# A two-layer mixer and a DiT-like block on one core: wider modulation sums, sums moved between the down rows, and products of constants at layer ends

## What is computed

```python
for l in range(2):                                   # first block
    h = x @ w_in[l]; ...                             # two attentions, gates
    x = layer_norm(ALPHA * x + merged @ w_out[l])
mod = silu(c) @ mod_w[i] + mod_b[i]                  # 9 vectors of 1024 per layer
h = x * (1 + scale) + shift                          # modulate
y = 0.5 * ((a * silu(g)) @ wo)                       # half FFN; a, g = h @ wi
x = layer_norm(ALPHA * x + gate * y)
```

## Time and profile before

| | |
|---|---|
| Median of 3 runs | 1699.57 us (1698.55 to 1700.25) |
| The profiled execution's own time | 1696.36 us |
| Its span, first to last instruction | 1694.6 us |
| PE busy | 1601.3 us (94%) |
| DVE busy | 1207.7 us (71%) |
| ACT busy | 802.3 us (47%) |
| Mean granted clock of TensorE | 0.971 |

### The profile page before, as it was taken

One profiled execution on the slowest core, in us unless ns is written; L12 is line 12 of the kernel. 1 busy time (PEld: TensorE's weight loads), 2 busy tenths in 40 slices (PEclk: granted clock), 3 DMA queues, 4 the chain that ended last, 5 costly groups with the idle time before them and its releaser, 6 DMA issues.

```text
span 1694.6 us, 23800 instructions
## 1 busy us (share of the span) xinstructions
PE 1601.3 (94%) x7635; PEld 1311.9 (77%) x7635; DVE 1207.7 (71%) x1849; ACT 802.3 (47%) x1242; POOL 140.1 (8%) x205
## 2 busy tenths in 40 slices
PE   6989989989889999999999798999999999989997
PEld 5877778877678878888788457887888878878876
DVE  6877888877887775677757766777487765475545
ACT  5565535455444444444534465444354443254442
POOL 1100001100011110011100011111001110000000
PEclk9999988999989999999999899999999999999999
DMA  8763448743568888588858105988768885466551
GB/s 313 270 208 128 150 152 310 249 169 112 175 219 267 275 270 233 163 280 275 228 181 243 50 1 173 308 275 270 206 212 275 276 232 176 124 177 196 184 183 55
DMA packets 200497, 349.41 MB, mean 206 GB/s; under 512 B 11188, under 2 KB 128236, under 8 KB 199900
## 3 DMA queue, kind: packets, MB, share of 16 engines
q1 hardware_dynamic: 174668, 252.90, 47.2%
q0 software_dynamic: 25744, 95.43, 17.6%
HBM read 347.21 MB, written 1.08 MB: 206 GB/s over the span
## 4 chain that ended last, share of the span: by engine, by line
PE 86%; DVE 8%; issue 3%; ACT 2%; DMA 0%; SPq 0%; DVEq 0%; ACTq 0%
PE acc L558 25%; PE acc L560 25%; PE acc L559 25%; DVE w_lo L1455 2%; PE score L682 2%; PE turn L886 1%; PE acc L794 1%; PE score L973 1%; PE score L670 1%; PE score L774 1%; DVE att_work L2007 1%; PE turn L783 1%; PE score L838 1%; DVE wide L1783 0%; PE score L577 0%
## 5 line engine op out<-in xcount | busy, mean ns | idle before, releaser
L1455 DVE TENSOR_TENSOR w_lo<-raw,w_hi 128x1024 fp32r<-128x1024 f32 (+1 forms) x490 | 586.0, 1200 | 294.3 <-ACT w_hi L1087 287.7
L1087 ACT ACTIVATE w_hi<-raw 128x1024 fp32r<-128x1024 f32 (+1 forms) x490 | 508.2, 1042 | 563.8 <-PE acc L560 561.4
L558 PE MATMUL acc<-w_hi,xT_hi 128*128 128x512 f32 (+1 forms) x1456 | 586.8, 403 | 23.1 <-DVE xT_lo L1502 8.5
L560 PE MATMUL acc<-w_hi,xT_lo 128*128 128x512 f32 (+1 forms) x1456 | 574.6, 395 | 0.0
L559 PE MATMUL acc<-w_lo,xT_hi 128*128 128x512 f32 (+1 forms) x1456 | 574.1, 394 | 0.0
L558 PEld LDWEIGHTS acc<-w_hi,xT_hi 128*128 128x128 f32 x1456 | 279.4, 192 | 83.1 <-issue 25.7
L560 PEld LDWEIGHTS acc<-w_hi,xT_lo 128*128 128x128 f32 x1456 | 278.6, 191 | 59.2
L559 PEld LDWEIGHTS acc<-w_lo,xT_hi 128*128 128x128 f32 x1456 | 279.6, 192 | 54.6
L458 POOL DMA_DIRECT2D mod_raw<-in_mod_w x144 | 104.0, 723 | 963.5 <-DVE mod_run L1575 777.4
L558 PE MATMUL acc<-w_hi,hT_hi 128*128 128x512 f32 x440 | 174.3, 396 | 0.8 <-DVE hT_lo L1916 0.8
L560 PE MATMUL acc<-w_hi,hT_lo 128*128 128x512 f32 x440 | 173.6, 395 | 0.0
(11 more groups left out here) (259 smaller groups left out, 1266.0 us busy)
## 6 DMA issues: line engine op xcount, KB each, us to landing
raw<-in_ffn_wi SPq DMA_DIRECT2D x220, 512.0 KB, 5.0
mod_raw<-in_mod_w POOLq DMA_DIRECT2D x144, 512.0 KB, 4.4
raw<-in_ffn_wo SPq DMA_DIRECT2D x110, 512.0 KB, 4.8
raw<-in_w_in SPq DMA_DIRECT2D x72, 512.0 KB, 5.2
raw<-in_w_out SPq DMA_DIRECT2D x16, 512.0 KB, 4.5
raw<-in_attn_wqkv SPq DMA_DIRECT2D x16, 512.0 KB, 4.6
wide<-in_b_merge POOLq DMA_DIRECT2D x4, 1024.0 KB, 8.3
raw<-in_w_branch_a SPq DMA_DIRECT2D x8, 512.0 KB, 4.2
```

Source lines behind the costliest of these rows:

```text
L558: nc.tensor.matmul(dst, xh, wh, start=start, stop=False)
L560: return nc.tensor.matmul(dst, xl, wh, start=False, stop=stop)
L1087: nc.scalar.activation(w_hi[:, i % SPLIT_SLOTS, 0:n], raw[:, s, i % 2 * PIECE:i % 2 * PIECE + n], ACT.Copy).then_inc(hi_ready, 1)
L1455: nc.vector.tensor_tensor(w_lo[:, i % SPLIT_SLOTS, 0:n], raw[:, i // 2 % RAW_SLOTS, i % 2 * PIECE:i % 2 * PIECE + n], w_hi[:, i % SPLIT_SL ...
```

## The change

Three parts, all on PE:

1. Every modulation sum multiplies by 48 columns of ones in place of one. The 48 results are equal, and the next product overwrites 47 of them, so that each column that is read holds its own sum. The bank, the count of products and the loads of weights stay.
2. In the first two FFNs the 24 kept sums no longer stand behind the last down row. Four of them follow each of the down rows 11 to 16.
3. A helper `keep_busy(b, n)` issues n products of 128 x 128 constants (`ident` by `ones`) into a free bank, and nobody reads them. At the start of both layers and of the first FFN: 5 ahead of the wait for tile 0, 10 ahead of the wait for tile 1, 5 behind the turn. In the third and fifth FFN, in `project_first`: 6 ahead of the turn of tile 0, 11 behind it, 6 ahead of the turn of tile 1. No such products stand at the start of the fourth FFN and of the Fourier mixing.

```diff
@@ turn @@
                     if tile_ready and g == 0:
+                        if wait[t]:
+                            keep_busy("acc0", wait[t])
                         tile_ready()
@@ project_first @@
+                if not kept:
+                    keep_busy("score0", 6)
                 slots, after = [], [turn_tile(0)]
                 if kept:
                     kept_sums(KEPT_EARLY, MOD_KEPT)
+                else:
+                    keep_busy("score0", 11)
...
                             if i == 2:
+                                if not kept:
+                                    keep_busy("score0", 6)
                                 after.append(turn_tile(1))
@@ new @@
+            def keep_busy(b, n):
+                landed(b)
+                for _ in range(n):
+                    nc.tensor.matmul(bank[b][:, 0:P], ident[:], ones[:], start=True, stop=True)
@@ mod_sum; the same in kept_sums @@
-                        m = nc.tensor.matmul(dst[:, 4 * i + j:4 * i + j + 1], acc[:, j * P:j * P + P], ones[:, 0:1],
+                        m = nc.tensor.matmul(dst[:, 4 * i + j:4 * i + j + SUM_COLS], acc[:, j * P:j * P + P], ones[:, 0:SUM_COLS],
@@ the loop over layers @@
-                after = turn(lambda t, k: x[:, t, k * P:k * P + P], x_tile)
+                after = turn(lambda t, k: x[:, t, k * P:k * P + P], x_tile, wait=(5, 10))
+                keep_busy("acc0", 5)
@@ ffn, down rows @@
                     m.then_inc(piece_done, 1)
+                    if mods and not by_tile and 0 <= k - KEPT_FROM < MOD_KEPT:
+                        kept_sums(k - KEPT_FROM, k - KEPT_FROM + 1)
...
-                if mods:
-                    kept_sums(0, KEPT_EARLY if by_tile else MOD_KEPT)
+                if mods and by_tile:
+                    kept_sums(0, KEPT_EARLY)
@@ the second block @@
-            after = ffn(turn_x(), True, turn_ctx_in, by_tile=False)
+            after = turn_x(wait=(5, 10))
+            keep_busy("acc0", 5)
+            after = ffn(after, True, turn_ctx_in, by_tile=False)
```

More of the change, by code:

```diff
@@ L77 @@
 KEPT_EARLY = 2
+SUM_COLS = 48
+KEPT_FROM = 11
 ACC = ["acc0", "acc1", "acc2", "acc3"]
@@ L560, in product, with turn @@
                 return nc.tensor.matmul(dst, xl, wh, start=False, stop=stop)
-            def turn(src, tile_ready=None, group_ready=None, groups=range(4)):
+            def turn(src, tile_ready=None, group_ready=None, groups=range(4), wait=(0, 0)):
                 order = [(t, g) for t in range(NT) for g in groups] if tile_ready else [(t, g) for g in groups for t in range(NT)]
@@ L681, in kept_sums @@
                     for j in range(4):
-                        m = nc.tensor.matmul(bank["score1"][:, 4 * i + j:4 * i + j + 1], mod_kept[:, i, j * P:j * P + P], ones[:, 0:1],
+                        m = nc.tensor.matmul(bank["score1"][:, 4 * i + j:4 * i + j + SUM_COLS], mod_kept[:, i, j * P:j * P + P], ones[:, 0:SUM_COLS],
                                              start=True, stop=True)
@@ L930, in ffn, with turn_x @@
                         m.then_inc(first_done, 1)
-                if mods:
-                    kept_sums(0, KEPT_EARLY if by_tile else MOD_KEPT)
-                return after
-            def turn_x():
-                return turn(lambda t, k: x[:, t, k * P:k * P + P], x_tile)
+                if mods and by_tile:
+                    kept_sums(0, KEPT_EARLY)
+                return after
+            def turn_x(wait=(0, 0)):
+                return turn(lambda t, k: x[:, t, k * P:k * P + P], x_tile, wait=wait)
             def turn_ctx_in():
```

## The result

The change is slower: 1703.22 us median against 1698.53 us for the kernel before, ratio 1.0028 (95% interval 1.0019 to 1.0037). The forecast was 1692.5 us. The profiled execution after takes 1704.65 us by its own time; that of before, 1696.36 us, was among the faster ones of its kernel, so the two traces lie 8.3 us apart where the medians lie 4.7. The ratios leave out an execution that lies far above all others of its kernel, as the one of 1837.81 us in the third experiment, which its median keeps. I follow the traces first and then say how much of it is the change and how much the execution.

A forecast was written before the change was run, and what follows sets the result against it. Low clock was taken to cost only where PE sets the pace, DVE's norm ending nearly all PE waits. Terms summed to 4.6 us off 1696.36, giving 1691.8; with 0.7 of offset, 1692.5 us, range 1686 to 1700.

The forecast's parts named there:

- Start: Products from 18.43 to 24.49 us regain the full clock: gain 2.3 us, bounds 1.5 and 2.8.
- Start of layer 2: Products from 257.70 to 263.43 regain full clock, less delay from ten constants: gain 1.5 us, bounds 0.5 and 1.9.
- Middle of the layers: Wide sums ahead of a wait keep the clock up in both layers: gain 1.3 us, bounds 0 and 2.6.
- First FFN: At its start, ten constants delay the turn, full-clock products gain 1.9 us: net -0.8, between +0.1 and -2.1.
- The moved sums: First and second FFN: waits for `acc1` and `w_lo` lose cover; 0.8 us lost together, bounds -4 and +1.
- Fourth FFN: Tile 1's x sets the turn, so 0; a clock fall costs up to 1.3 us; taken -0.3.
- Fourier: PE was late for tile 1's turn behind 32 slow sum records; up to 1.7 us return, taken 1.4.
- The offset: Timed runs before lie 2.2 to 3.9 us above the profiled execution; 0.7 of 3.2 carried into the forecast.
- The 49 us: Whole kernel: mean clock 0.971 over 1694.6 us equated with 49 us at 1.2 GHz in place of 2.4.
- rival C: Whole kernel: all low-clock time returns, 49 us, giving 1650 us; chance 0.03.
- Rival A: Waits swallow the gain, DVE sets the time nearly everywhere, new seam waits lose the clock: 1699 us; chance 0.17.
- Rival B: Constants run at half clock and delay the turns (layer 2, FFNs), ten taking 4.4 us: 1711 us; chance 0.08.

The follow-up runs named there:

- e3: Kernel before with only the constant products at the turns (start of both layers and first FFN) added; 1701.95 us, ratio 1.0022.
- e5: Kernel before with only the constant products in `project_first` (third and fifth FFN) added; 1698.61 against 1698.58 us, ratio 0.9997.
- c13: The change itself, timed again beside other kernels on the same chip; 1701.69 us, ratio 1.0016 to the kernel before.
- e6: The change with the first feature of the second modulation block one split later on DVE; 1699.22 us, ratio 1.0007 to the kernel before.
- e9: The change without the ten constant products ahead of tile 1's turn, fives kept; 1697.21 us, ratio 0.9996 to the kernel before.
- e4: Kernel before with its sums widened to 128 columns and nothing else; 1688.19 us, ratio 0.9932.
- c14: The change with its kept sums back behind the last down row, timed beside the change itself; 1691.36 us, ratio 0.9955 to the kernel before.
- c15: The change without the constant products of `project_first` (third and fifth FFN); 1702.37 us, ratio 1.0020 to the kernel before.
- e1: Kernel before with its sums widened to 48 columns and nothing else; 1695.08 us against 1700.12, ratio 0.9970.
- e2: Kernel before with sums of 48 columns and the kept sums moved between the down rows, no constants; 1698.89 us, ratio 0.9993.
- e12: The change with its kept sums back behind the last down row, first timing; 1695.16 us, ratio 0.9979 to the kernel before.
- c16: The change with kept sums back in place and without the ten constants ahead of tile 1's turns; 1690.98 us, ratio 0.9950 to the kernel before.

## Why the prediction was wrong

The direction was wrong, and the range (1686 to 1700) did not hold 1703.2.

- **Start, +2.3, "bounds 1.5 and 2.8".** This step failed. The 2.7 us were there by piece 2, at full clock from the first product; some 0.8 of them the trace of e5 has without constants. But the term ended there. I looked at 18 to 24 us and asked only whether DVE would be late; I never asked what the lead would run into. It ran into the load of `mod_raw`, which came at 50.8 to 52.4 us in every trace but that of before, with a split behind it in DVE's list. It cost 5.3 us by piece 14 in this trace and 3.5 in c13's (-2.79 to +0.73), where 2.1 to 2.4 are the lead lost in the wait for `mod_raw` and the rest a fall of the clock in that wait. The row was in reach: `mod_raw` had already made DVE wait 0.60 us at 49.72, with DMA engines at 1.03. The lower bound should have been below zero.
- **Start of layer 2, +1.5.** Pieces 59 to 62 gained 1.7, so the term was right where it looked, and had the same hole behind it: 3.5 lost by piece 74. The later order on DVE (e6) removes that loss.
- **Middle of the layers, +1.3.** Layer 1 gained 1.3 in the products behind 188.93, layer 2 nothing. Right. Another 1.1 us came at pieces 52 and 53 of layer 1, which had no term.
- **First FFN, -0.8.** The ten ran at full clock; +0.3 in the trace, inside its +0.1 to -2.1 but for 0.2. The delay of the turn, 1.6 of the forecast 1.8, is real, and the kernel without the ten (e9) did better.
- **The moved sums, -0.8 for both, bounds -4 and +1.** Mechanism right to the tenth: a wait of 3.12 us for `acc1` (3.1 forecast), the first of the two `w_lo` done 6.4 us behind the last down row (694.95 to 701.3). Size off: -1.6 and -1.4 in place of -0.4 each, since the clock fell in the wait, which I had priced at "some 1.5 more" and left out of the likeliest value. The larger error was in what it was held against. I set the move against the seam of before, 11.3 us. What the move gives up is the seam with wide sums left in place, 8.1 us (e4, c14). I had that number and wrote that "the bank excludes" it; the bank excludes it only because the sums were moved.
- **Third and fifth FFN, 0.** Right (e5, c15).
- **Fourth FFN, -0.3.** -1.3 in the trace from the fall in the longer wait, the bound of the text.
- **Fourier, +1.4.** +1.25 at that place. Right.
- **No term** stood for a loss of 1.6 at pieces 28 and 29 (new stretch of 0.50 from 114.35, in the scores of layer 1), which c13 lacks and e5 has, so it is not the change's. Nor did one stand for the 1.9 us from piece 253 to 264, which are in every trace of the change.
- **The offset.** I carried 0.7 of the 3.2 us between the profiled execution and the median of before, thinking that the change would take most falls away. It did halve the time at 0.50, twelve stretches of 51 us together against fifteen of 102, but new ones stand where PE sets the pace, behind its waits for `mod_raw` and in the scores.
- **The 49 us.** The opening of the prediction calls 0.971 the same as 49 us at 1.2 GHz. Work at 1.2 GHz loses half its time, so it is some 98 us at 1.2 GHz (the trace has 102), of which 49 would be lost. Only rival C uses the number, and uses it as the loss.
- **The whole.** Forecast was +4.6, the trace has -8.3. Of the 12.9 between, 4.9 stand at the start, 3.3 at the start of layer 2, 2.2 at the seams, 1.9 and 1.6 at the two places without a term and 1.0 in the fourth FFN; the first FFN and pieces 52 and 53 came out 1.1 better each, and the rest is the Fourier's and rounding.

Rival A came nearest: waits swallow the gain and the new waits lose the clock. It stopped at "no change" as it had nothing for the load of `mod_raw`. Rival B's clock did not fall under the ten in this trace or in c13's; in c14's it did, at 4.47 us for them where B had 4.4.

The parts by their own timings: wide sums -0.30% (e1), sums moved +0.23% (e2 less e1), constants at the turns +0.22% (e3), `project_first` -0.03% (e5). Their sum is +0.12%, against +0.28 and +0.16 (c13) measured; each has an interval of 0.1 to 0.2% to either side, so this neither bears out nor excludes a loss from the parts together.

## What to carry to other kernels

A gain at one place is a lead, and a lead has to be followed to the next thing that does not move with it. Here that was a load that landed at about the same time however far PE was ahead, with the DMA engines full (share 1.0): the lead turned into a wait and was gone, and where the clock fell in that wait PE left the place later than before. When one change both makes a piece of work better cover and moves it out of the wait it covered, price the two apart: here the first was worth 5 to 12 us, and the second gave back 4 to 10. A higher mean clock is no result; look at whether PE works or waits in the stretches that rose.

## What the runs showed of the hardware

- Sums of 128 columns cost 0.110 us a record (5.28 us for 48), no more than 48 columns (696.83 - 691.56 = 5.27 for 48), and the clock stayed full under them in all five traces, where it fell under 48 columns in e1, e12 and c16 and held in c14. Widening from 48 to 128 was worth 6.9 us. I had expected 0 to 2.
- The same program on the same chip has executions 7 us apart (c14: 1690.61 to 1697.52) and the profiled one may be at either end. Which places show 0.50 differs between them: c13, the change again, had 3.4 us at half near 52 us where the first trace had 6.8. A sum made from one trace of this kernel carries some 3 us of that.
- DVE had `mod_raw` at 49.7 us in before and at 50.8 to 52.4 in the nineteen other traces, with PE 0.4 to 2.9 us ahead at piece 2 (50.8 at 0.4 in e4, 51.2 at 0.8 in e5, 50.9 at 2.9 in c16): on full DMA engines its time does not follow the lead. The trace of before was the odd one: e5, the same program up to there, had 51.2.
- Products of constants did not bring back a clock that had fallen just ahead of them. The ten of the first FFN took 2.40 us in the change and 4.47 in c14, which has the same code there; both began behind a wait of PE of 3.10 us, in which the clock fell in c14 alone.
